# Value products of the first chunk ahead of the second gate pair in a decoder layer kernel: a change in the order of work

## Chip, cores and metric

One core of one Trainium2 chip runs the whole kernel. The metric is the time of one execution in microseconds, as the median of the runs; lower is better.

## What is computed

One decoder layer, in fp32, for a prompt of 256 tokens and eight sample sequences of one token each with 1024 cached tokens (8 pages of 128):

```
x = x + 0.5 * g1 * SwiGLU_1(mod1(rmsnorm(x)))
h = mod2(rmsnorm(x)); [qA|kA|vA|qB|kB|vB|gA|gB] = h @ w_in
  branch A: 8 heads x 64, blocks of 256, top-3 past blocks + own block
  branch B: 4 heads, q/k halves of 64, value 128, w = p0 - lam * p1, sub-RMSNorm
x = x + g2 * ((sig(gA) * yA + sig(gB) * yB) @ w_out)
x = x + 0.5 * g3 * SwiGLU_2(mod3(rmsnorm(x)))
```

In both branches the sample's token also attends to its own new key and value ("own products" below: q times own k). The model width is 1024, the feed-forward width 2816. The pages of keys and values are found through a table.

## The kernel before

Everything is held feature-major: 264 columns (256 prompt tokens and 8 sample tokens) by 1024 features in eight chunks of 128. A weight arrives in blocks of 1 MB in four buffers (`raw`). ScalarE rounds a half block to `whi` (the function `hi`), VectorE or GpSimd (POOL) computes the rest `wlo` (`lo`, L1055 on VectorE, L662 on POOL), and TensorE multiplies three times for each pair of 128x128 tiles: whi with hhi, whi with hlo, wlo with hhi (L1611 to L1613; in the later gates L1959 to L1961). A half block of 24 such products is one "half"; there are 20 halves from the keys and values to the first two gate blocks, numbered 0 to 19 (`kv_product(g)`, halves 16 to 19 are the gates' first two blocks, called W_GATE and W_GATE+1).

Every engine has its order of work written out by hand, and semaphores tie them together. The order around the change is this.

- **The loop over u = 0 to 16 on TensorE** computes half u, turns keys and values of earlier halves, and scores cached keys: `scores(0, u + 2)` for branch A and `scores(1, u)` for branch B, where one step is half a sequence (4 pages). Each needs its page block turned by VectorE in 32x32 tiles (`turn_keys`, L1266). At u = 12 it also multiplies the own products (tile `ev`, L1935) that VectorE made in `own_products` (L1294, L1299); the result goes into the sample's maxima.
- **VectorE beside it** turns the key blocks, and does the sample's softmax for two groups of four sequences, e = 0 and 1: `sample_logits` (block sums and distances), `sample_ranks` (the ranks of the blocks and the maximum, L1323 to L1348, after TensorE's `block_sums`, L1890), and, after ScalarE's exponentials (`sample_exp`, L868, L870) and TensorE's `exp_sums` (L1895), `sample_scale` (L1356 to L1363), which scales and turns the weights. TensorE turns them once more (`turn_probs`, L1904), and ScalarE copies them out (`turned_probs`) and into padded tiles (`pad_weights`, tile `wpad`, L952).
- **The loop over c = 0 to 7** has one chunk each: the cached values' products of one sequence (L1994; two half sequences of two branches, each 4 page products), the turn of the prompt's probabilities (L2022), the prompt's scores of the next chunk (L1910, L1911), halves of the later gates in chunks 1 to 6 (`gate_half`) and the prompt's output (L2044, L2045). VectorE has `prompt_logits` (L1376 to L1381) and `prompt_scale` (L1390 to L1401), ScalarE `prompt_exp` (L936, L938).
- **The page blocks** ("uses" 0 to 31, 16 of keys and then 16 of values, 1 MB for each branch and use) go through three buffers for each branch. SyncE (SP) loads branch A and the weights, POOL loads branch B (both L473). A load waits until the products of the use that had its buffer are done. The table `AHEAD` says behind which use SP asks for which weight block (L545).
- **POOL** also computes the rest of halves 5 to 19 in the same list as its loads.

Of the kernel before, what the change touches and what calls it, by code (L numbers as in the profile page):

```python
# [211 lines left out]
def build(nc, A, O):  # L212
    ctx = ExitStack()
    with ctx:
# [285 lines left out]
        def filler(k):  # L500

            return W_KV + k // 2, k % 2
# [7 lines left out]
        def turn_bank(c, h):  # L510
# [6 lines left out]
                 18: [W_GATE + 2, W_GATE + 3, W_GATE + 4], 19: [W_GATE + 5], 21: [W_GATE + 6], 23: [W_GATE + 7], 25: [W_BR]}  # L517
# [105 lines left out]
        def _(pool):  # L623
# [41 lines left out]
            for use in range(KVS + 2, 4 * TS):  # L665
                kv_load(pool, 1, use)
                if 6 <= use <= 11:
                    lo(*filler(use - 1))
                if 11 <= use < POOL_HALVES - 1:
                    lo(*filler(use))  # L670
                if use == POOL_HALVES - 2:
                    lo(*filler(use + 1))
                if use in K_ROWS:
                    i = K_ROWS[use]
                    pool.wait_ge(s_tok, 4 * (i + 1))
                    row_out("k", i // 2, i % 2, ktok, ktoks, s_krow)
                if use in V_ROWS:
                    i = V_ROWS[use]
                    pool.wait_ge(s_vtok, 4 * (i + 1))
                    row_out("v", i // 2, i % 2, vtok, vtoks, s_vrow)  # L680
# [15 lines left out]
        def _(a):  # L696
# [259 lines left out]
            for t in range(2):  # L956
                hi(W_GATE + 2, t)
# [3 lines left out]
            pad_weights(1)  # L961
            gate_pair(1)
            npp = 0
            sample_exp(1)
            for c in range(KC):
                gated = 1 <= c <= 6
                if c == 1:
                    turned_probs(1)
# [15 lines left out]
                if c + 1 < KC:  # L984
                    pad_weights(2 * c + 2)
                    pad_weights(2 * c + 3)
                    prompt_exp(c + 1)
                if gated:
                    gate_half(c + 1, 1)
# [55 lines left out]
        def _(v):  # L1045
# [432 lines left out]
            for c in range(KC):  # L1478
# [15 lines left out]
                if c == 0:  # L1494
                    sample_scale(1)
# [107 lines left out]
        def _(pe):  # L1603
# [309 lines left out]
            for u in range(2 * TS + 1):  # L1913
# [17 lines left out]
                if u == 12:  # L1931
# [31 lines left out]

            kv_product(17)
            kv_product(18)
            turn_probs(0)
# [13 lines left out]
            npp = 0  # L1980
            for c in range(KC):
# [5 lines left out]
                w0 = 24 - 8 * (c % 4)  # L1987
                for half in range(2):
                    pe.wait_ge(s_wpad, 2 * c + half + 1)
                    for ab in range(2):  # L1990
                        use = 16 + 2 * c + half
                        pe.wait_ge(kv_sem(ab, use), kv_landed(ab, use))
                        for q in range(4):
                            ins = mm(bank[32 * q:32 * q + 32, 4 + ab, :], wpad[half][:, q, ab, w0:w0 + 32], kv_slot(ab, use)[:, q, :],  # L1994
                                     start=(half == 0 and c % 4 == 0), stop=(half == 1 and q > 0 and c % 4 == 3))
                        ins.then_inc(s_pv, 1)
                    if half == 0 and c == 1:
                        turn_probs(1)
# [4 lines left out]
                    if half == 1 and c == 0:  # L2003
                        exp_sums(1)
# [7 lines left out]
                for h in range(2 if c < 4 else 1):  # L2012
# [4 lines left out]
                    if (c, h) == (0, 1):  # L2017
                        pe.wait_ge(s_sig, 2)
                    if (c, h) == (1, 1):
                        pe.wait_ge(s_pTs, 2)  # L2020
# [4 lines left out]
                if c + 1 < KC:  # L2025
                    pe.wait_ge(s_plog, 2 * c + 2)
                    if c == 0:
                        pe.wait_ge(s_sig, 1)
                    prompt_scores(c + 1)
# [16 lines left out]
                ins.then_inc(s_po, 1)  # L2046
                if c % 4 == 3:
# [86 lines left out]
```

## Time and profile before

| | |
|---|---|
| median of 3 runs | 769.61 us (768.85 to 771.45) |
| profiled execution: its time | 771.59 us |
| its span, first to last instruction | 769.9 us |
| mean granted TensorE clock | 0.984 |
| busy PE, DVE, ACT, POOL | 95%, 61%, 43%, 16% |
| read from HBM | 205.33 MB, 271 GB/s over the span |

The profile is of one execution. Busy shares are of its span, and positions in it are in microseconds from the span's start. A matmul's duration overlaps with its neighbours', so a group's cost is read from start to start. The stage that the change touches lies between about 360 and 450 us. A wait is shown behind an instruction in brackets: how long the engine was idle and who released it.

### The profile page before, as it was taken

The numbers are of one execution on the slowest core, as the hardware profiler recorded it, in microseconds if no ns is written. First come the engines' busy times: TensorE is split into PE (matmuls) and PEld (weight loads), VectorE is DVE, ScalarE is ACT, GpSimd is POOL, SyncE is SP. The second block draws the span as 40 slices with busy tenths as digits, with TensorE's granted clock in tenths as the row PEclk, the third lists the DMA queues.
The fourth block names the chain that finished last, engine by engine and source line by source line (L and its number), as shares of the span: only waits on it lengthen the run. The fifth ranks groups of instructions, "written<-read, shape, count | busy, mean of one in ns | idle before, by whom it ended". The sixth has DMA issues, their size and how long they took to land.

```text
span 769.9 us, 17290 instructions
## 1 busy us (share of the span) xinstructions
PE 734.7 (95%) x6732; PEld 654.3 (85%) x6732; DVE 467.9 (61%) x699; ACT 334.2 (43%) x568; POOL 123.7 (16%) x179
## 2 busy tenths in 40 slices
PE   5899999999999999998999699999989999999997
PEld 2398998999999799998886366669979999999997
DVE  2664445455354879978998255778676545545451
ACT  2453333344343643554255254475554434434431
POOL 0000000002000422787665223210000000000000
PEclk9999999999999999999899899999999999999999
DMA  9978989987986599999988998996517566555520
GB/s 353 375 245 271 323 288 317 331 263 293 393 273 203 234 391 381 375 389 390 368 315 280 404 401 300 356 346 224 165 55 218 165 184 193 168 172 183 185 91 29
DMA packets 116521, 209.57 MB, mean 272 GB/s; under 512 B 6714, under 2 KB 100186, under 8 KB 104162
## 3 DMA queue, kind: packets, MB, share of 16 engines
q1 hardware_dynamic: 106784, 159.47, 60.5%
q0 software_dynamic: 9440, 49.04, 16.4%
q8 instruction: 47, 0.77, 0.4%
q14 instruction: 24, 0.20, 0.1%
q10 hardware_dynamic: 226, 0.10, 0.0%
HBM read 205.33 MB, written 3.24 MB: 271 GB/s over the span
## 4 chain that ended last, share of the span: by engine, by line
PE 77%; DVE 11%; DMA 6%; issue 2%; ACT 2%; SPq 2%; ACTq 0%; DVEq 0%
PE bank L1611 21%; PE bank L1612 20%; PE bank L1613 20%; DMA early<-in_w_ada 3%; PE bank L1994 3%; PE bank L1860 2%; DMA kvA_lent<-in_cache_v_moba 2%; PE bank L1667 2%; PE bank L1959 1%; DMA kvA<-in_cache_k_moba 1%; PE bank L1960 1%; PE bank L1961 1%; DVE kvB L1266 1%; DVE wlo L1055 1%; SPq L473 1%
## 5 line engine op out<-in xcount | busy, mean ns | idle before, releaser
L1055 DVE TENSOR_TENSOR wlo<-raw,whi 128x1024 fp32r<-128x1024 f32 (+1 forms) x177 | 208.6, 1199 | 175.5 <-ACT whi L711 172.7
L1611 PE MATMUL bank<-hhi,whi 128*128 128x264 f32 x992 | 287.3, 290 | 3.6 <-DVE wlo L1055 2.0
L1612 PE MATMUL bank<-hlo,whi 128*128 128x264 f32 x992 | 282.6, 285 | 0.0
L1613 PE MATMUL bank<-hhi,wlo 128*128 128x264 f32 x992 | 282.0, 284 | 0.0
L711 ACT ACTIVATE whi<-raw 128x1024 fp32r<-128x1024 f32 (+1 forms) x192 | 194.5, 1034 | 105.8 <-PE bank L1613 70.4
L1611 PEld LDWEIGHTS bank<-hhi,whi 128*128 128x128 f32 x992 | 188.1, 190 | 15.9 <-issue 13.6
L1612 PEld LDWEIGHTS bank<-hlo,whi 128*128 128x128 f32 x992 | 188.3, 190 | 0.1
L1613 PEld LDWEIGHTS bank<-hhi,wlo 128*128 128x128 f32 x992 | 187.4, 189 | 0.0
L1611 PE MATMUL bank<-ahi,whi 128*128 128x264 f32 x416 | 119.8, 288 | 0.4 <-DVE alo L1569 0.4
L1613 PE MATMUL bank<-ahi,wlo 128*128 128x264 f32 x416 | 118.2, 284 | 0.0
L1612 PE MATMUL bank<-alo,whi 128*128 128x264 f32 x416 | 117.6, 283 | 0.0
L1611 PEld LDWEIGHTS bank<-ahi,whi 128*128 128x128 f32 x416 | 78.3, 188 | 0.8 <-DVE alo L1569 0.6
L1612 PEld LDWEIGHTS bank<-alo,whi 128*128 128x128 f32 x416 | 78.3, 188 | 0.2
L1613 PEld LDWEIGHTS bank<-ahi,wlo 128*128 128x128 f32 x416 | 78.3, 188 | 0.0
L745 ACT ACTIVATE sil<-bank 128x528 f32<-128x528 f32 x22 | 13.5, 612 | 74.5 <-PE bank L1613 74.5
L749 ACT ACTIVATE ahi<-act 128x528 f32 (+1 forms) x22 | 14.2, 646 | 53.8 <-DVE act L1141 53.8
L662 POOL TENSOR_TENSOR wlo<-raw,whi 128x1024 fp32r<-128x1024 f32 x15 | 35.8, 2388 | 1.9 <-ACT whi L711 1.3
L473 POOL DMA_DIRECT2D kvB<-in_cache_v_diff x44 | 23.3, 530 | 42.4 <-PE bank L1994 34.0
L1959 PE MATMUL bank<-hhi,whi 128*128 128x264 f32 x96 | 28.5, 297 | 0.0
L1145 DVE TENSOR_TENSOR alo<-act,ahi 128x528 f32 (+1 forms) x22 | 15.6, 709 | 19.3 <-ACT ahi L749 19.3
L1960 PE MATMUL bank<-hlo,whi 128*128 128x264 f32 x96 | 27.2, 284 | 0.0
L1961 PE MATMUL bank<-hhi,wlo 128*128 128x264 f32 x96 | 27.2, 283 | 0.0
(284 smaller groups left out, 825.6 us busy)
## 6 DMA issues: line engine op xcount, KB each, us to landing
raw<-in_ffn_w_gate SPq DMA_DIRECT2D x22, 1024.0 KB, 5.4
raw<-in_ffn_w_up SPq DMA_DIRECT2D x22, 1024.0 KB, 5.5
raw<-in_w_ada SPq DMA_DIRECT2D x20, 1024.0 KB, 7.0
raw<-in_w_in SPq DMA_DIRECT2D x20, 1024.0 KB, 10.6
raw<-in_ffn_w_down SPq DMA_DIRECT2D x16, 1024.0 KB, 5.1
kvA<-in_cache_v_moba SPq DMA_DIRECT2D x44, 256.0 KB, 6.3
kvB<-in_cache_v_diff POOLq DMA_DIRECT2D x44, 256.0 KB, 5.9
kvA<-in_cache_k_moba SPq DMA_DIRECT2D x36, 256.0 KB, 6.6
```

Of the source, the lines that this page charges most:

```text
L473: eng.dma_start(rows_, cache[bass.ds(page, 1)].rearrange("a (j t) d -> (a j) (t d)", t=4)).then_inc(kv_sem(ab, use), 16)
L662: nc.gpsimd.tensor_tensor(half_view(wlo[n % 2], key, t), half_view(raw[s], key, t), half_view(whi[n % 2], key, t).bitcast(F32), ALU.subtra ...
L711: nc.scalar.activation(half_view(whi[key[1] % 2], key, t), half_view(raw[s], key, t), ACT.Copy).then_inc(s_hi, 1)
L1055: dve.tensor_tensor(half_view(wlo[key[1] % 2], key, t), half_view(raw[s], key, t), half_view(whi[key[1] % 2], key, t).bitcast(F32), ALU.su ...
L1145: dve.tensor_tensor(alo[:, bass.ds(2 * i, 2), :], act[:, :, :], ahi[:, bass.ds(2 * i, 2), :].bitcast(F32), ALU.subtract).then_inc(s_alo, 1)
L1611: mm(out, wh, xh, start=start, stop=False)
L1612: mm(out, wh, xl, start=False, stop=False)
L1613: return mm(out, wl, xh, start=False, stop=stop)
L1959: mm(out, wh, hhi[:, k, :], start=(k == 0), stop=False)
L1960: mm(out, wh, hlo[:, k, :], start=False, stop=False)
L1961: ins = mm(out, wl, hhi[:, k, :], start=False, stop=(k == KC - 1))
L1994: ins = mm(bank[32 * q:32 * q + 32, 4 + ab, :], wpad[half][:, q, ab, w0:w0 + 32], kv_slot(ab, use)[:, q, :], start=(half == 0 and c % 4 == ...
```

## The change

It moves work in the lists of all engines; nothing is added or left out, but for one wait on POOL.

1. TensorE multiplies the own products at u = 13 instead of 12, behind half 13 and the turn of the values.
2. TensorE turns the first four sequences' weights right behind half 17, ahead of half 18, and does chunk 0's value products (a new function `values`) behind half 18, ahead of `block_sums(1)` and half 19.
3. In chunk 0 TensorE scores the prompt's second chunk between the two turns of the prompt's probabilities, and does `exp_sums(1)` last, behind the prompt's output.
4. The second four sequences' exponentials (ScalarE) stand behind the prompt's exponentials of chunk 1 instead of ahead of the loop; `sample_scale(1)` on VectorE stands in chunk 1 instead of 0; `turn_probs(1)` on TensorE in chunk 2 instead of 1, and ScalarE's copy too.
5. ScalarE rounds W_GATE+2 behind the padding of the weights instead of ahead of it.
6. POOL waits for the first scaled weights before it computes the rest of half 19.
7. Four blocks of gate and branch weights are asked for behind the page block that they stood ahead of.

```diff
-                 18: [W_GATE + 2, W_GATE + 3, W_GATE + 4], 19: [W_GATE + 5], 21: [W_GATE + 6], 23: [W_GATE + 7], 25: [W_BR]}
+                 18: [W_GATE + 2, W_GATE + 3, W_GATE + 4], 20: [W_GATE + 5], 22: [W_GATE + 6], 24: [W_GATE + 7], 26: [W_BR]}
...
                 if use == POOL_HALVES - 2:
+                    pool.wait_ge(s_pscaled, 1)
                     lo(*filler(use + 1))
...
             gate_pair(0)
-            for t in range(2):
-                hi(W_GATE + 2, t)
             turned_probs(0)
             a.wait_ge(s_wzero, 1)
             pad_weights(0)
             pad_weights(1)
+            for t in range(2):
+                hi(W_GATE + 2, t)
             gate_pair(1)
             npp = 0
-            sample_exp(1)
...
-                if c == 1:
+                if c == 2:
                     turned_probs(1)
...
                     prompt_exp(c + 1)
+                if c == 0:
+                    sample_exp(1)
...
-                if c == 0:
+                if c == 1:
                     sample_scale(1)
...
-                if u == 12:
+                if u == 13:
                     pe.wait_ge(s_ecur, 1)
...
+            def values(c, half):
+
+                w0 = 24 - 8 * (c % 4)
+                pe.wait_ge(s_wpad, 2 * c + half + 1)
+                for ab in range(2):
+                    use = 16 + 2 * c + half
+                    pe.wait_ge(kv_sem(ab, use), kv_landed(ab, use))
...
             kv_product(17)
+            turn_probs(0)
             kv_product(18)
-            turn_probs(0)
+            values(0, 0)
+            values(0, 1)
             block_sums(1)
             kv_product(19)
...
-                    if half == 0 and c == 1:
+                for half in range(2 if c else 0):
+                    values(c, half)
+                    if half == 0 and c == 2:
                         turn_probs(1)
...
-                    if half == 1 and c == 0:
-                        exp_sums(1)
...
                     if (c, h) == (0, 1):
+                        prompt_scores(1)
                         pe.wait_ge(s_sig, 2)
+                    if (c, h) == (1, 1):
+                        pe.wait_ge(s_pscaled, 2)
...
                 ins.then_inc(s_po, 1)
+                if c == 0:
+                    exp_sums(1)
```

The order of instructions shows it at three places. The first is TensorE behind half 18, before (L1904 is the turn of the weights, L1890 the block sums, the rows behind are half 19):

```order
L1613 MATMUL bank<-hhi,wlo_57 128x264
L1904 MATMUL bank<-prob_117,const 32x128 [waits probs_scaled]
L1904 MATMUL bank<-prob_117,const 32x128 x15
L1890 MATMUL bank<-sm,const 128x8 [waits block_parts]
L1611 MATMUL bank<-hhi,whi_55 128x264 [waits lo_ready,v_tokens_ready]
```

and now (L1974 are the value products, L1892 the block sums):

```order
L1615 MATMUL bank<-hhi,wlo_57 128x264
L1974 MATMUL bank<-kvA_97,wpad_142 32x512 [waits kv_landedA1,weights_padded]
L1974 MATMUL bank<-kvA_97,wpad_142 32x512 x3
L1974 MATMUL bank<-kvB_99,wpad_142 32x512 [waits kv_landedB1]
L1974 MATMUL bank<-kvB_99,wpad_142 32x512 x3
L1974 MATMUL bank<-kvA_lent,wpad_143 32x512 [waits kv_landedA2,weights_padded]
L1974 MATMUL bank<-kvA_lent,wpad_143 32x512 x3
L1974 MATMUL bank<-kvB_lent,wpad_143 32x512 [waits kv_landedB2]
L1974 MATMUL bank<-kvB_lent,wpad_143 32x512 x3
L1892 MATMUL bank<-sm,const 128x8 [waits block_parts]
L1613 MATMUL bank<-hhi,whi_55 128x264 [waits lo_ready,v_tokens_ready]
```

The turn is gone from here (it stands ahead of half 18), and eight rows of value products stand between half 18 and the block sums of the second four sequences.

The second is TensorE at the end of chunk 0, before (L1895 are the exponentials' sums, L2022 the turns of the prompt's probabilities, L1910 and L1911 the scores, L2044 and L2045 the output):

```order
L1994 MATMUL bank<-kvB_lent,wpad_143 32x512 x3
L1895 MATMUL bank<-sm,const 128x2 [waits probs_ready]
L2022 MATMUL bank<-const,plog_129 128x128 [waits prompt_probs]
L2022 MATMUL bank<-const,plog_129 128x128 x2
L2022 MATMUL bank<-const,plog_130 128x128 [waits gate_out,prompt_probs]
L2022 MATMUL bank<-const,plog_130 128x128 x2
L1910 MATMUL bank<-kT,qT 128x128 [waits gate_out,prompt_logits]
L1911 MATMUL bank<-kT,qT 128x256
L1910 MATMUL bank<-kT,qT 128x128
L1911 MATMUL bank<-kT,qT 128x256
L2044 MATMUL bank<-pts_131,vtok 64x256 [waits prompt_probs_ready]
L2045 MATMUL bank<-pts_131,vtok 64x128
```

and now (L1897 the sums, L2033 the turns, L1912 and L1913 the scores, L2053 and L2054 the output, L1974 chunk 1's values):

```order
L1912 MATMUL bank<-kT,qT 128x128
L1913 MATMUL bank<-kT,qT 128x256
L2033 MATMUL bank<-const,plog_130 128x128 [waits gate_out]
L2033 MATMUL bank<-const,plog_130 128x128 x2
L2053 MATMUL bank<-pts_131,vtok 64x256 [waits prompt_probs_ready]
L2054 MATMUL bank<-pts_131,vtok 64x128
L2053 MATMUL bank<-pts_132,vtok 64x256
L2054 MATMUL bank<-pts_132,vtok 64x128
L1897 MATMUL bank<-sm,const 128x2 [waits probs_ready]
L1974 MATMUL bank<-kvA_96,wpad_142 32x512 [waits kv_landedA0,weights_padded]
L1974 MATMUL bank<-kvA_96,wpad_142 32x512 x3
```

The sums, with their wait for the exponentials, have gone from the head of the chunk to its end, and chunk 1's values stand behind them.

The third is ScalarE in the same place, before (L868 and L870 are the second group's exponentials, L936 and L938 the prompt's):

```order
L925 ACTIVATE gT<-bank 128x528 [waits gemm_done]
L868 ACTIVATE prob_118,sm<-prob_118,mxt_123 128x256 [waits logits_ready]
L868 ACTIVATE prob_118,sm<-prob_118,mxt_123 128x256
L870 ACTIVATE ncur<-ncur 128x2
L983 ACTIVATE pts_131<-bank 128x384 [waits prompt_probs_turned]
L983 ACTIVATE pts_132<-bank 128x384 [waits prompt_probs_turned]
L952 ACTIVATE wpad_142<-probT_119 128x8x8 [waits v_used,probs_turned_ready]
L952 ACTIVATE wpad_143<-probT_119 128x8x8 [waits v_used,probs_turned_ready]
L936 ACTIVATE plog_129,stat<-plog_129,stat,qroot 128x128 [waits prompt_logits]
L938 ACTIVATE plog_129,stat<-plog_129,stat,qroot 128x256
L936 ACTIVATE plog_130,stat<-plog_130,stat,qroot 128x128 [waits prompt_logits]
L938 ACTIVATE plog_130,stat<-plog_130,stat,qroot 128x256
```

and now (L869 and L871, L937 and L939):

```order
L926 ACTIVATE gT<-bank 128x528 [waits gemm_done]
L983 ACTIVATE pts_131<-bank 128x384 [waits prompt_probs_turned]
L983 ACTIVATE pts_132<-bank 128x384 [waits prompt_probs_turned]
L953 ACTIVATE wpad_142<-probT_119 128x8x8 [waits v_used,probs_turned_ready]
L953 ACTIVATE wpad_143<-probT_119 128x8x8 [waits v_used,probs_turned_ready]
L937 ACTIVATE plog_129,stat<-plog_129,stat,qroot 128x128 [waits prompt_logits]
L939 ACTIVATE plog_129,stat<-plog_129,stat,qroot 128x256
L937 ACTIVATE plog_130,stat<-plog_130,stat,qroot 128x128 [waits prompt_logits]
L939 ACTIVATE plog_130,stat<-plog_130,stat,qroot 128x256
L869 ACTIVATE prob_118,sm<-prob_118,mxt_123 128x256 [waits logits_ready]
L869 ACTIVATE prob_118,sm<-prob_118,mxt_123 128x256
L871 ACTIVATE ncur<-ncur 128x2
```

The sample's exponentials have gone behind those of the prompt's second chunk.

## Rows read from the trace of the kernel before

**Rows 1.** The page's chain of work that ended last, shares of the span by engine

```profile
PE 77%; DVE 11%; DMA 6%; issue 2%; ACT 2%; SPq 2%; ACTq 0%; DVEq 0%
```

**Rows 2.** Windows: busy us (instructions) PE, PEld, DVE, ACT, POOL; PEclk, DMA share, GB/s

```profile
360.00:370.00 10.00, 6.32 (x57) 5.95 (x61) 9.96 (x12) 1.80 (x4) 7.24 (x10) 0.82 1.02 413
380.00:390.00 10.00, 9.94 (x129) 8.70 (x129) 9.65 (x16) 6.08 (x14) 9.86 (x13) 1.00 0.97 348
```

**Rows 3.** TensorE's timeline from 367 us: start, duration, instruction, [idle before, releaser]

```profile
367.32 1.86 PE L1935 MATMUL bank<-const,ev 128*128 128x1 f32 x8 [3.68 <-DVE ev L1299]
...
370.82 1.93 PE L1860 MATMUL bank<-kvB,qrow 128*32 128x128 f32 x32
372.68 0.59 PE L1611 MATMUL bank<-hhi,whi 128*128 128x264 f32 x1
```

**Rows 4.** VectorE's timeline from 365 us, same columns

```profile
365.00 1.38 DVE L1294 TENSOR_TENSOR stat<-qT,kT 128x32 f32<-128x32 f32 x2
...
381.04 2.67 DVE L1343 TENSOR_TENSOR mxt<-mxt,ncur 128x2 f32<-128x2 f32 x1
...
384.77 2.30 DVE L1266 STREAM_TRANSPOSE kvB<-kvB 128x2048 f32<-128x2048 f32 x1
```

**Rows 5.** POOL's timeline at 381 us, same columns

```profile
381.30 2.37 POOL L662 TENSOR_TENSOR wlo<-raw,whi 128x1024 fp32r<-128x1024 f32 x1
```

**Rows 6.** TensorE's timeline from 387 to 411 us

```profile
387.13 1.08 PE L1860 MATMUL bank<-kvB,qrow 128*32 128x128 f32 x32
...
398.06 1.08 PE L1904 MATMUL bank<-prob,const 128*32 128x128 f32 x32 [0.39 <-DVE prob L1360]
400.20 0.39 PE L1890 MATMUL bank<-sm,const 128*128 128x8 f32 x2 [1.05 <-DVE prob L1315]
...
405.06 1.06 PE L1994 MATMUL bank<-kvA,wpad 128*32 128x512 f32 x8
...
408.63 0.38 PE L1895 MATMUL bank<-sm,const 128*128 128x2 f32 x2
...
411.33 1.06 PE L1994 MATMUL bank<-kvA,wpad 128*32 128x512 f32 x8
```

**Rows 7.** VectorE's timeline from 401 to 415 us

```profile
401.38 0.16 DVE L1323 COPY sm<-bank 128x8 f32<-128x8 f32 x1
...
406.06 2.36 DVE L1055 TENSOR_TENSOR wlo<-raw,whi 128x1024 fp32r<-128x1024 f32 x2
...
411.69 0.73 DVE L1376 SCALAR_TENSOR_TENSOR plog<-const,qroot,bank 128x128 f32<-128x128 f32 x2
...
414.88 0.16 DVE L1381 SCALAR_TENSOR_TENSOR stat<-stat,qroot 128x2 f32<-128x2 f32 x1
```

**Rows 8.** ScalarE's timeline from 406 to 416 us

```profile
406.14 0.51 ACT L868 ACTIVATE prob<-prob,mxt 128x256 f32<-128x256 f32 x1 [0.36 <-DVE ncur L1348]
...
407.14 0.19 ACT L870 ACTIVATE ncur<-ncur 128x2 f32<-128x2 f32 x1
...
416.06 0.19 ACT L938 ACTIVATION_READ_ACCUMULATOR plog<-plog,stat,qroot 128x1 f32 x1
```

**Rows 9.** SyncE's timeline of transfer issues from 408 us

```profile
408.82 0.58 SPq L545 DMA_DIRECT2D raw<-in_w_in  x1
412.19 2.53 SPq L473 DMA_DIRECT2D kvA_lent<-in_cache_v_moba  x4
```

**Rows 10.** The chain of waits in order of time: start, duration, what

```profile
414.19 16.83 DMA kvA_lent<-in_cache_v_moba
431.15 3.64 PE bank L1994 x16
...
446.30 1.85 PE bank L1994 x16
```

**Rows 11.** Windows of one microsecond at two places, columns of rows 2

```profile
403.00:404.00 1.00, 1.00 (x7) 1.00 (x6) 0.93 (x3) 0.00 (x0) 0.00 (x0) 0.51 0.00 0
431.00:432.00 1.00, 0.85 (x5) 0.25 (x9) 0.00 (x0) 0.00 (x0) 0.00 (x0) 0.50 0.99 365
```

More of the change, by code:

```diff
@@ L1962, in gate_half @@
                 ins.then_inc(s_gemm, 1)
+            def values(c, half):
[4 more added lines that the diff above has]
+                    pe.wait_ge(kv_sem(ab, use), kv_landed(ab, use))
+                    for q in range(4):
+                        ins = mm(bank[32 * q:32 * q + 32, 4 + ab, :], wpad[half][:, q, ab, w0:w0 + 32], kv_slot(ab, use)[:, q, :],
+                                 start=(half == 0 and c % 4 == 0), stop=(half == 1 and q > 0 and c % 4 == 3))
+                    ins.then_inc(s_pv, 1)
             kv_product(17)
+            turn_probs(0)
             kv_product(18)
-            turn_probs(0)
+            values(0, 0)
+            values(0, 1)
             block_sums(1)
@@ L1980, in _ @@
             npp = 0
+            pe.wait_ge(s_plog, 2)
+            pe.wait_ge(s_sig, 1)
             for c in range(KC):
@@ L1986, in _ @@
                 gated = 1 <= c <= 6
[L1987 to L1996, printed above, removed]
-                    if half == 0 and c == 1:
+                for half in range(2 if c else 0):
+                    values(c, half)
+                    if half == 0 and c == 2:
                         turn_probs(1)
@@ L2017, in _ @@
                     if (c, h) == (0, 1):
+                        prompt_scores(1)
                         pe.wait_ge(s_sig, 2)
                     if (c, h) == (1, 1):
+                        pe.wait_ge(s_pscaled, 2)
+                    if (c, h) == (2, 1):
                         pe.wait_ge(s_pTs, 2)
@@ L2024, in _ @@
                     npp += 1
-                if c + 1 < KC:
+                if 1 <= c < KC - 1:
                     pe.wait_ge(s_plog, 2 * c + 2)
-                    if c == 0:
-                        pe.wait_ge(s_sig, 1)
                     prompt_scores(c + 1)
```

## Prediction

> **What bounds the kernel now.** I read the chain of waits of the page first: it follows TensorE for 77% of the span, VectorE for 11% and DMA for 6% [rows 1]. The change touches the mixing stage; the feed-forward stages before and after it are TensorE's own, and a microsecond won or lost in the stage should reach the end whole. So the question is what ends the waits in that stage.
>
> The windows come next [rows 2]: in the ten microseconds from 360 TensorE is busy 6.32 of 10 and VectorE 9.96; from 380 VectorE still has 9.65. In VectorE's timeline there is no idle entry at all from 352 to 408 us. TensorE's first wait, 3.68 us for the block-spread own products (tile ev), ends at 367.32 [rows 3]; what follows runs at the lower clock, thirty-two score products in 1.93 us, and the product at 372.68 still takes 0.59 us. But this wait is where TensorE catches up with VectorE, not what holds VectorE.
>
> VectorE's timeline says why [rows 4]: own products from 365.00, the last key block turned at 384.77, 2.30 us. In between a 128x2 maximum took 2.67 us at 381.04; a POOL subtraction of 128x1024 runs beside it from 381.30 for 2.37 us [rows 5], and the small operation ends when POOL's does. Six such operations stand between 365 and 397.
>
> From 387.13 TensorE is the slower one again [rows 6]: scores, three gate products, a wait of 0.39 us before the turn of the weights (398.06), one of 1.05 us before the block sums (400.20), then four value half-blocks from 405.06 to 408.63, and those of chunk 1 from 411.33.
>
> **Part 1: own products one step later, priced at nothing.** Eight small products move behind the next projection. TensorE no longer waits 3.68 us at 363.6, nor pays the low clock there. But the scores of the last key half wait for VectorE's turn that begins at 384.77 and ends at 387.07, and VectorE's list up to there is the same, with nothing in it that waited for TensorE. So I expect TensorE to reach those scores about 6 us early and to stand still until 387.1: the wait is moved, not removed. Its cover is that VectorE stays busy; bounds are a gain of 2.4 us (below, first rival) and a loss of 0.4 us, should POOL's earlier subtraction catch one more small operation.
>
> The moved wait costs something new. In the kernel before TensorE came to those scores at full clock (1.08 us [rows 6]). After six idle microseconds it will restart at half. The price comes from the other long wait of this trace: sixteen value products took 3.64 us behind it and 1.85 us elsewhere, and the half clock ended there, so 1.8 us. Bounds: 0, and 2.9 us, half of the 5.8 us from 367.32 to about 373.1. I take **+1.8 us**, since that wait was as long.
>
> **Part 2: turn and values ahead of the second gate pair's last half.** Before, 13.07 us pass from the scores (387.13) to the block sums (400.20). The waits of 0.39 and 1.05 go, since VectorE's scaled weights (398.0 before) now meet a TensorE that is 1.8 us later and still has a projection in between; the added wait on POOL keeps its last subtraction off that scaling, worth up to 2 us to VectorE, all of it hidden. Behind that wait in POOL's order stand the stores of value rows and the next page loads; those pages are read 20 us later, so nobody waits for them. Added ahead of the block sums are the values, 408.63 - 405.06 = 3.6 us. Block sums: 387.13 + 13.07 - 1.44 + 3.57 + 1.8 = **404.1**, 3.9 us later than before.
>
> **Part 3: the second four sequences' chain.** This is where it hurts. Behind the block sums VectorE has the ranks (401.38 to 406.06, 4.7 us), the low part of a gate weight (2.36 us) and now at once chunk 1's prompt logits (411.69 to 415.04, 3.35 us) [rows 7]. ScalarE then has the prompt's exponentials, ended 1.2 us later, and only behind them the sample's exponentials, 406.14 to 407.33, 1.2 us [rows 8]. The exponentials' sums on TensorE wait for that, and chunk 1's values stand behind them in TensorE's order. With 0.45 us for the block sums and 0.35 us for the sums: 0.45 + 4.7 + 2.36 + 3.35 + 1.2 + 1.2 + 0.35 = 13.6 us. So chunk 1's values start at 404.1 + 13.6 = **417.7**, against 411.33: 6.4 us later. TensorE has only some 6.5 us of work for these 13.6 (a projection, six turns, scores, prompt output), so it stands about 7 us and restarts at half clock once more, **+1.8 us** (bounds 0 and 2.9). ScalarE's two high parts of that weight also move, behind the padding; they are done before the ranks and cost nothing.
>
> **Part 4: pages earlier, weights later.** Before, SP issues a gate weight at 408.82 ahead of the value pages of 412.19 [rows 9], and TensorE stands 6.5 us until the last of those pages, 16.83 us on its way, is there at 431.02 (414.19 + 16.83); then come the 3.64 us at low clock [rows 10]. The granted clock was 0.51 at 403 to 404 and 0.50 at 431 to 432 [rows 11], the lower of the two levels (1.2 of 2.4 GHz); the first of these windows also shows the queues empty, 0 GB/s: no buffer was free. Now chunk 0's values free two pairs of buffers at about 402 and 404, and with no weight in front the page pair is issued at once: even with 16.8 us on its way it lands near 423. Both the 6.5 us and the 1.8 us of low clock go. The turn of the second probabilities (1.1 us) leaves chunk 1 and enters chunk 2: nothing. The later weights have at least a chunk until they are read: nothing.
>
> **Sum, at chunk 2's values.** Chunk 1 took 431.15 - 6.5 - 411.33 = 13.3 us. After: 417.7 + 13.3 - 1.1 + 1.8 = 431.7, against 431.15: +0.6. Behind it -1.8 (no low clock) and +1.1 (the turn): -0.1 us. **Five microseconds won at each end are spent in the middle: no change.** The profiled execution took 771.59 us (span 769.9), so 771.5 by its own clock; it stands 2.0 us above the median of the runs, 769.61, and I forecast for the median **769.5 us**.
>
> What this measurement can tell from no change is 0.3%, 2.3 us.
>
> **Rivals.**
> - *VectorE gets faster (0.31).* POOL's subtractions follow TensorE's scores through the buffers, so they come some 6 us earlier. Should one fall on the turn of the key block, which the subtractions do not lengthen (2.3 us with and without), instead of on the ranks, VectorE is 2.4 us earlier at 384.8, and everything behind with it: 769.5 - 2.4 = 767.1. For it: I place the subtraction for the eighteenth half at 381.5, one microsecond before the ranks would end unhindered. Against it: at 381.5 it hits. With full clock at the first restart as well, 765.3.
> - *The low clock lasts longer at both restarts (0.14).* If it ends as late as at 373.1 rather than as at 434.8, each restart costs 2.9 us instead of 1.8: 769.5 + 2.2 = 771.7, slower. It decides from where light products (scores, 32 columns) fill the first microseconds, as they do at the first restart; at the second, values of the kind that 3.64 us shows come first, which speaks against it there.
> - *The page wait moves one half on (0.10).* The next pages can only be asked for behind chunk 1's first values, 419.4 to 421.9. If the last of them is again 16.8 us on its way, it lands at 438.7; chunk 1 and the first half of chunk 2 need them at 431.7 + 1.8 + 1.1 + 3.0 = 437.6. A wait of 1.1 us and some low clock, 1.8 at most: 772.4, slower. It decides from 15.7 us on the way; against it, only some 5 MB will be asked for at that point at the 413 GB/s of [rows 2].
>
> **What would show it.** Right: TensorE idle about 6 us before the last key scores, which start within 0.5 us of 387; granted clock 0.5 behind it; block sums near 404; a wait of about 7 us before L1897 that ends on ScalarE's L871; no DMA wait at chunk 2's values, which start near 431.7. Wrong: key scores at 385 (VectorE faster, first rival), no wait at L1897 (my chain is too long), or a wait for kvA or kvB pages in chunk 2.

## The result, and the profile after

The changed kernel took 775.82 us (median of 7 runs, 772.82 to 777.81), the kernel before beside it 771.18 us (7 runs, 765.92 to 771.46). The ratio is 1.0068, with an interval of 1.0037 to 1.0098: slower by about 5 us, where no change was forecast (769.5 us, range 765.3 to 772.4). Timed once more later, it was 776.81 against 771.45 us (below), so the loss is the kernel's own.

The page's share line of the chain, of the changed kernel, answers to [rows 1]: DMA has gone from 6% to 3%, and TensorE from 77% to 82%.

```profile
PE 82%; DVE 11%; DMA 3%; ACT 2%; issue 2%; SPq 1%; ACTq 0%; DVEq 0%
```

TensorE's timeline of the changed kernel from 368 us (start, duration, instruction, [idle before, releaser]), beside [rows 3, 6]:

```profile
368.70 0.95 PE L1937 MATMUL bank<-const,ev 128*128 128x1 f32 x8
...
387.65 0.66 PE L1862 MATMUL bank<-kvB,qrow 128*32 128x128 f32 x8 [6.92 <-DVE kvB L1268]
...
401.50 1.07 PE L1974 MATMUL bank<-kvA,wpad 128*32 128x512 f32 x8
...
405.07 0.39 PE L1892 MATMUL bank<-sm,const 128*128 128x8 f32 x2
...
418.29 0.59 PE L1897 MATMUL bank<-sm,const 128*128 128x2 f32 x2 [6.70 <-ACT ncur L871]
418.81 1.93 PE L1974 MATMUL bank<-kvA,wpad 128*32 128x512 f32 x8
...
433.23 1.07 PE L1974 MATMUL bank<-kvA_lent,wpad 128*32 128x512 f32 x8
```

The picture is the one drawn in advance. The wait of 3.68 us before the own products (L1937, tile `ev`) is gone; one of 6.92 us stands before the last key scores. A wait of 6.70 us on ScalarE's L871 stands before the exponentials' sums. No wait for a page is left. Chunk 2's values start at 433.23, forecast 431.7. Behind the second wait eight value products take 1.93 us, against 1.07 us later on.

The windows of the changed kernel (columns of [rows 2]) show the granted clock in both waits, and again where the loop over the chunks ends:

```profile
386.00:387.00 1.00, 0.00 (x0) 0.00 (x0) 1.00 (x1) 1.00 (x6) 0.00 (x0) 0.50 1.03 387
414.00:415.00 1.00, 0.00 (x0) 0.00 (x0) 0.95 (x4) 0.64 (x3) 0.00 (x0) 0.50 1.09 442
505.00:512.00 7.00, 6.42 (x32) 3.68 (x22) 3.90 (x6) 3.75 (x6) 1.45 (x2) 0.74 0.94 332
512.00:519.00 7.00, 7.00 (x32) 6.82 (x33) 3.69 (x6) 4.79 (x7) 1.42 (x2) 0.52 0.93 339
```

and the last two windows in the kernel before, which [rows 11] did not hold:

```profile
505.00:512.00 7.00, 6.42 (x33) 4.72 (x32) 3.56 (x7) 4.13 (x9) 2.75 (x4) 0.84 0.94 305
512.00:519.00 7.00, 7.00 (x55) 7.00 (x55) 6.05 (x9) 4.43 (x7) 0.13 (x1) 0.91 1.00 364
```

The order of work there is the same in both kernels. Read in windows of one microsecond, the low clock lasts 10.2 us in the changed kernel (from 508 us) and 3.4 us in the kernel before (from 509 us). The forecast had not looked there.

To compare places I count from TensorE's branch B scores of half 11 (358.91 us before, 358.04 after), since executions enter the stage up to 4 us apart. The columns are microseconds from there; each comes from the starts in one profile. A chunk's column is the start of its value products, "page wait" the wait for a page in chunk 2, and "end" the end of the span.

| profile | last key scores | chunk 1 | chunk 2 | chunk 3 | end | page wait |
|---|---|---|---|---|---|---|
| before | 28.2 | 52.4 | 72.2 | 87.3 | 411.0 | 6.50 |
| before, 2nd | 28.3 | 52.5 | 69.7 | 84.5 | 409.7 | 3.89 |
| before, 3rd | 28.5 | 51.6 | 69.3 | 84.3 | 411.2 | 4.00 |
| change | 29.6 | 60.8 | 75.2 | 89.4 | 416.1 | none |
| change, 2nd | 29.6 | 60.8 | 75.2 | 89.5 | 416.1 | none |
| change, 3rd | 29.6 | 61.0 | 75.6 | 89.9 | 416.6 | none |

The kernel before differs from itself by 3 us at chunk 3, the changed one by 0.5 us. The profile that the forecast was worked out from is the kernel before with its longest page wait.

### The profile page after: what moved, and what is told of

It reads as the page before. It is cut to its first block, busy times and chain, and to the rows that moved or that the text cites. A ratio compares the mean times of both kernels' runs of the same rounds, so it can differ in the third digit from the quotient of the medians.

```text
span 774.1 us, 17290 instructions
## 1 busy us (share of the span) xinstructions
PE 736.2 (95%) x6732; PEld 655.5 (85%) x6732; DVE 468.6 (61%) x699; ACT 333.8 (43%) x568; POOL 123.4 (16%) x179
## 4 chain that ended last, share of the span: by engine, by line
PE 82%; DVE 11%; DMA 3%; ACT 2%; issue 2%; SPq 1%; ACTq 0%; DVEq 0%
PE bank L1613 22%; PE bank L1614 21%; PE bank L1615 21%; PE bank L1974 3%; PE bank L1862 3%; DMA early<-in_w_ada 3%; PE bank L1669 2%; PE bank L1961 1%; PE bank L1962 1%; PE bank L1963 1%; DVE wlo L1057 1%; DVE kvB L1268 1%; DVE prob L1342 1%; PE bank L2063 1%; DVE kvB_lent L1268 1%
## 5 line engine op out<-in xcount | busy, mean ns | idle before, releaser
L1613 PEld LDWEIGHTS bank<-hhi,whi 128*128 128x128 f32 x992 | 188.3, 190 | 16.5 <-issue 13.6
```

The costliest lines, as they stand in the source:

```text
L1613: mm(out, wh, xh, start=start, stop=False)
```

## The experiments

Two theories stood after the result, and the expectations call them A and B. **Theory A**: the loss lies in the stage, in TensorE's two new waits, in the chain on other engines that ends them, and in the restarts at low clock behind them. **Theory B**: the loss comes from the low clock at the end of the loop, whatever the stage does. The first four runs undo one part of the change each; the kernel before beside these four took 770.75 us (35 runs). "The change" is the first series, 775.82 us; it was not timed beside them, but the fourth run, as slow as the change, was.

### The sums later

`exp_sums(1)` leaves the end of chunk 0 and stands behind chunk 1's values.

```diff
+                if c == 1:
+                    exp_sums(1)
...
-                if c == 0:
-                    exp_sums(1)
```

> The changed kernel with the second group's exponential sums behind chunk 1's values instead of at the end of chunk 0. Theory A (the wait for them, 6.7 us, and the restart at half clock behind it are on the path): chunk 1's values start near 412 instead of 418.8, at full clock; 7 to 9 us faster than the changed kernel, less what the pages of use 20 and 21 then make TensorE wait; so 2 to 4 us faster than the kernel before. Theory B (the loss comes from the clock at the end of the loop, near 509 us, whatever the stage does): at most 2 us from the changed kernel, with a long low spell there again.

774.32 us (12 runs), ratio 1.0055 (1.0029 to 1.0082). Its timeline of TensorE:

```profile
426.41 0.88 PE L2035 MATMUL bank<-const,plog 128*128 128x128 f32 x3 [5.00 <-DVE prob L1362]
```

Chunk 1's values start 54.4 us after the reference score instead of 60.8, but chunk 2's at 73.8 instead of 75.2. The wait moved on to the next thing that needs VectorE's scaled weights, and kept 5.0 of its 6.7 us. The wait at the sums was the chain's, not the sums' own. Theory A's figure, 7 to 9 us faster, missed for that: 1.5 us came out, at chunk 3 too (88.0 instead of 89.4), and the low clock at the loop's end lasted 10.2 us again. By itself this run does not tell A from B.

### Block sums ahead of chunk 0's values

```diff
+            block_sums(1)
             values(0, 0)
             values(0, 1)
-            block_sums(1)
```

> The changed kernel with the second group's block sums ahead of chunk 0's values. Theory A: VectorE's ranks start 3.6 us earlier, the wait for the exponentials shrinks from 6.7 to about 3.1 us, and the restart may stay cold: 3 to 5 us faster than the changed kernel. Theory B: no change beyond 1 us in the stage's part, and the end of the loop decides.

772.65 us (12 runs), ratio 1.0026 (0.9999 to 1.0054): 3.2 us less than the change. The wait before the sums is 4.34 us instead of 6.70:

```profile
416.77 0.59 PE L1897 MATMUL bank<-sm,const 128*128 128x2 f32 x2 [4.34 <-ACT ncur L871]
```

The values had stood in the way of the chain that the next chunk waits for. Chunk 3's values start at 87.2 instead of 89.4, so 2.2 of the 3.2 us are seen in the stage, which theory B did not allow. By the medians this order is about two thirds of the loss; the interval, 0.9999 to 1.0054, is wide beside that.

### Own products back

```diff
-                if u == 13:
+                if u == 12:
```

> The changed kernel with the own products at step 12 as before. Theory A (VectorE sets when the last key scores start; the moved wait only costs a restart at half clock there): key scores still start near 387.5 but at full clock, so 1.5 to 2.5 us faster than the changed kernel. Rival (the move is a gain): 3 to 6 us slower.

772.6 us (12 runs), ratio 1.0027 (1.0 to 1.0053): 3.2 us less than the change too. Its last key scores come at 28.5 instead of 29.6 and at full clock (1.08 us), and chunk 3's values at 87.4 instead of 89.4. The two gains of 3.2 us together are more than the whole loss, so each is known only roughly.

### The old table of weights

The line of `AHEAD` as it was before.

> The changed kernel with the gate weights asked for as before. If the early values alone took the page wait away, no change (within 1 us) and no wait for kvA_lent at chunk 2. If the order of the queue did it, a wait of 3 to 7 us is back at chunk 2's values and the kernel is 3 to 8 us slower.

776.13 us (12 runs), ratio 1.0086 (1.0054 to 1.0119): as the change. Its profile, of the fastest of the twelve (771.59 us), has no page wait either, so the new table is not needed for that. Nor were the pages asked for earlier. SyncE's timeline here, beside 412.19 in the kernel before [rows 9]:

```profile
414.99 2.46 SPq L473 DMA_DIRECT2D kvA_lent<-in_cache_v_moba  x4
```

From the reference score that is 57.2 us, against 53.3 in the kernel before. But they landed 3.8 to 4.2 us after their issue, against 13.2 to 16.8 in the first profile of the kernel before, and TensorE came for them at 74.2, 2 us behind even the longest wait's end (72.2). With the early values the loads are spread otherwise; that this made them quick is likely and not shown by itself.

The next two do one part alone, from the kernel before (768.16 us beside them, 23 runs); both kernels were also profiled again there, unedited.

### The new table alone

> The kernel before with the new prefetch table alone. Page block 20 goes ahead of a weight of 1 MB. If the queue's order makes the page wait, it shrinks by 2 us or more, and the kernel is 1 to 5 us faster than before; if the wait comes from buffers that come free late, it stays, and the time is the same within 1 us.

769.31 us (12 runs), ratio 1.0008 (0.9983 to 1.0033): nothing. In its profile the page wait is 2.00 us and stands before another page, that of chunk 2's second half:

```profile
428.48 1.61 PE L1994 MATMUL bank<-kvA,wpad 128*32 128x512 f32 x8 [2.00 <-DMA kvA<-in_cache_v_moba]
```

The profile is of the fastest of the twelve (765.45 us): chunk 3's values start at 80.8 there, 3.5 us ahead of any profile of the kernel before. Its wait can't be laid against theirs as the table's doing. So neither expectation is met whole: the wait is another one, and the time is the same.

### Own products later, alone

> The kernel before with the own products one step later, alone. Theory A (VectorE sets when the last key scores start, so the wait only moves): a wait of about 6.9 us ahead of the last key scores in place of 3.7 us ahead of the own products, a restart at half clock behind it, and 1 to 3 us slower than before. Rival (a real gain): 3 us or more faster.

772.79 us (12 runs), ratio 1.0047 (1.0019 to 1.0075): 4.6 us above the kernel before beside it. The wait is the change's:

```profile
387.73 1.93 PE L1860 MATMUL bank<-kvB,qrow 128*32 128x128 f32 x32 [6.96 <-DVE kvB L1266]
```

Theory A had 1 to 3 us. The interval reaches from 1.5 to 5.8 us, and the profile shows less: chunk 3's values start at 85.3, within the 84.3 to 87.3 of the kernel before, and the span ends at 412.3. What is clear is that the last key scores come at 29.6 instead of 28.2 to 28.5, as in the change. The reason is on VectorE. The changed kernel there:

```profile
378.55 4.77 DVE L1342 TENSOR_TENSOR prob<-prob,sm 128x256 f32<-128x256 f32 x2
383.35 0.69 DVE L1344 TENSOR_REDUCE mxt<-prob 128x2 f32<-128x512 f32 x1
384.07 0.16 DVE L1345 TENSOR_TENSOR mxt<-mxt,ncur 128x2 f32<-128x2 f32 x1
...
385.29 2.31 DVE L1268 STREAM_TRANSPOSE kvB<-kvB 128x2048 f32<-128x2048 f32 x1
```

with POOL beside it:

```profile
378.52 2.13 POOL L473 DMA_DIRECT2D kvB_lent<-in_cache_v_diff  x4
380.67 2.35 POOL L662 TENSOR_TENSOR wlo<-raw,whi 128x1024 fp32r<-128x1024 f32 x1
```

and the same two products in the kernel before, with POOL's load beside them and the subtraction that follows the one of 381.30 [rows 5]:

```profile
379.40 0.89 DVE L1340 TENSOR_TENSOR prob<-prob,sm 128x256 f32<-128x256 f32 x2
...
379.02 2.26 POOL L473 DMA_DIRECT2D kvB<-in_cache_v_diff  x4 [0.86 <-PE bank L1860]
...
387.06 2.40 POOL L662 TENSOR_TENSOR wlo<-raw,whi 128x1024 fp32r<-128x1024 f32 x1
```

The two subtractions near 381 us are not of the same half. POOL makes fifteen, for halves 5 to 19. In the kernel before, 381.30 is the twelfth, of half 16, and 387.06 that of half 17; in the changed kernel 380.67 is the thirteenth, of half 17. So the subtraction of half 17 came 5.5 us earlier, counted from the reference score (28.15 to 22.63), and took the place in time that half 16's had held (22.39). VectorE's two products of L1342 now end with it: 4.77 us instead of 0.89. The maximum behind them falls from 2.67 us [rows 4] to 0.16, so the net is 1.4 us on the turn of the key block. All three profiles of the change show 4.77 or 4.78 us, and this one 4.50; with the own products back it is 0.89. The subtraction by itself, 2.35 us, costs no more than in the kernel before; what is new is that VectorE is held from about 379.0, 1.7 us before it begins. POOL was issuing a page load then, but the kernel before had such a load beside the same products (379.02 to 381.28) and they were not held. What held them in the change stays open.

### The kernel before, again

> The kernel before, once more under the profiler. If the wait of 6.5 us for value pages at chunk 2 belongs to the kernel, it is here again, 5 us or more. If it was a matter of that one execution, it is under 3 us here, and the change then has little to give back at that place, which would explain most of the 5 us that it costs.

770.38 us. Neither expectation came: the page wait is between the two, and the low clock behind it lasts 3.4 us, where the first profile has 6.8:

```profile
428.71 1.93 PE L1994 MATMUL bank<-kvA_lent,wpad 128*32 128x512 f32 x8 [3.89 <-DMA kvA_lent<-in_cache_v_moba]
```

### The change, again

> The changed kernel once more under the profiler. The waits ahead of the last key scores (6.9 us) and ahead of the exponentials' sums (6.7 us) come from the order of the work and stand here within 0.3 us. The low clock behind chunk 7 (508 to 518 us) is expected to differ in length if it depends on where in the execution it falls, and to be 10 us again if it belongs to the order.

780.05 us. It entered the stage 4.1 us later than the first profile and then kept its pace to 0.1 us (table above), with waits of 6.96 and 6.71 us. Between these two profiles the stage is not where the changed kernel varies. The low clock at the loop's end lasts 10.2 us again.

### All that helped, together

From the change: own products at u = 12, block sums ahead of chunk 0's values, the exponentials' sums behind chunk 1's first values and gate half, and, not tried alone, VectorE's `sample_scale(1)` in chunk 0 ahead of its next low part.

```diff
-                if c == 1:
-                    sample_scale(1)
...
+                if c == 0:
+                    sample_scale(1)
...
-                if u == 13:
+                if u == 12:
...
+            block_sums(1)
             values(0, 0)
             values(0, 1)
-            block_sums(1)
...
+                    if half == 0 and c == 1:
+                        exp_sums(1)
...
-                if c == 0:
-                    exp_sums(1)
```

> The changed kernel with four of its steps put otherwise: own products at step 12 again, the second block sums ahead of chunk 0's values, the exponentials' sums inside chunk 1 (behind the first gate half), the second scaling on VectorE ahead of the next weight's low part. By theory A (chain behind the block sums, and the restarts) nothing waits 6.7 us any more: counted from the score product of half 11, chunk 3's values start at 79 to 81 us (84.5 and 87.3 in the kernel before, 89.4 in the changed one), and the kernel is 3 to 6 us faster than before. By the rival (the early values themselves cost the time) it is no faster than before.

764.18 us (6 runs, 762.27 to 765.65) against 770.87 us, ratio 0.991 (0.9887 to 0.9934): **faster than both kernels**, 11.6 us below the change. TensorE's timeline has one long wait left in the stage, the old one for `ev`, and 1.56 us before the turn of the weights:

```profile
366.29 1.83 PE L1937 MATMUL bank<-const,ev 128*128 128x1 f32 x8 [3.68 <-DVE ev L1301]
...
395.61 1.08 PE L1906 MATMUL bank<-prob,const 128*32 128x128 f32 x32 [1.56 <-DVE prob L1362]
```

Chunk 2's values start 64.9 us after the reference score, 4.4 to 7.3 us ahead of the kernel before. Chunk 3's are at 79.1, inside theory A's 79 to 81; the rival, that the early values themselves cost the time, falls. So a kernel with the early values can be faster than the kernel before, once the work around them stands otherwise. How much of the 6.7 us is theirs, and how much is that of VectorE's earlier scaling, no run separates.

### POOL's wait left out

```diff
-                    pool.wait_ge(s_pscaled, 1)
```

> The changed kernel without POOL's added wait. Both theories: VectorE's scaling may be held 2 us by POOL's last subtraction, but TensorE comes to the turn of the weights later than that, so no change within 1 us, and the same waits of 6.9 and 6.7 us.

776.69 us (12 runs, one of which took 1440.17 us for a cause not known and is left out of the ratio), ratio 1.0072 (1.0049 to 1.0095): as the change. POOL's last subtraction starts only when ScalarE has rounded:

```profile
396.84 2.39 POOL L662 TENSOR_TENSOR wlo<-raw,whi 128x1024 fp32r<-128x1024 f32 x1 [1.33 <-ACT whi L711]
```

and VectorE's scaling was done by 393.1, so here the wait would have had nothing to hold.

### Work in the waits, too much of it

To price the restarts, TensorE gets products of constants into a bank that is overwritten afterwards, ahead of the last key scores and of the exponentials' sums, 14 in each. They are added work and part of no result.

```diff
+                if u == 15:
+                    pe.wait_ge(s_vtok, 10)
+                    for _ in range(14):
+                        mm(bank[:, 0, :], C("ones"), const[:, 0:512], start=True, stop=True)
...
                 if c == 0:
+                    for _ in range(14):
+                        mm(bank[:, 3, :], C("ones"), const[:, 0:512], start=True, stop=True)
                     exp_sums(1)
```

> The changed kernel with 14 products of constants in each of the two long waits of TensorE (ahead of the last key scores, and ahead of the exponentials' sums), written to a bank that nobody reads; they add work that the kernel does not need. The waits themselves stay, now filled. If restarting at half clock costs what the first profile shows, scores and values behind them run at full clock (1.08 us and 1.06 us instead of 1.94 and 1.93), and the kernel is 3 to 5 us faster than the changed one, that is about as fast as before. If the clock behind the waits costs nothing, no change within 1 us, or 1 us slower.

781.06 us (5 runs), ratio 1.013 (1.0104 to 1.0155). The 14 products took 12.2 us, not the 7 us of the wait:

```profile
380.77 12.18 PE L1944 MATMUL bank<-const 128*128 128x512 f32 x28
392.88 1.08 PE L1862 MATMUL bank<-kvB,qrow 128*32 128x128 f32 x32
```

The key scores started 5 us late for that, so this run says nothing of the price: mine was the mistake, an fp32 product of 512 columns is two records of 0.44 us each, start to start.

### The kernel before, a third time

> The kernel before a third time under the profiler. The page wait at chunk 2's values was 6.5 and 3.9 us in the two profiles so far. If it varies with the execution, a third value, between 0 and 7 us; the other waits (3.7, 0.4 and 1.05 us) stand within 0.1 us.

771.63 us, page wait 4.00 us. The other waits are 3.68, 0.53 and 1.05 us, so all but the second stand within 0.1 us. Of the three profiles only the first has more than 4 us at the page.

### Work in the waits, of the right size

The same with `range(7)` in both places, so 6.1 us of work in waits of 6.9 and 6.7; the change beside it, unedited, and the kernel before at 771.45 us (23 runs).

> The change with 7 instead of 14 products of constants in each of TensorE's two long waits, so 6.1 us of work (in the run with 14 they took 12.2 us) in waits of 6.9 and 6.7 us. If the two restarts at half clock cost about 2.5 us each, the last key scores start near 387.7 as in the change, both low stretches behind the waits are gone, and the time is some 4 to 6 us below the change beside it. If the low clock costs nothing and only the waits count, the two low stretches go and the time stays within 1 us of the change beside it.

771.43 us (12 runs), ratio 1.0007 (0.9981 to 1.0033). TensorE's timeline:

```profile
382.83 6.17 PE L1944 MATMUL bank<-const 128*128 128x512 f32 x14
389.93 1.08 PE L1862 MATMUL bank<-kvB,qrow 128*32 128x128 f32 x32 [0.93 <-DVE kvB L1268]
...
411.66 6.28 PE L2062 MATMUL bank<-const 128*128 128x512 f32 x14
418.45 0.38 PE L1897 MATMUL bank<-sm,const 128*128 128x2 f32 x2 [0.51 <-ACT ncur L871]
418.76 1.07 PE L1978 MATMUL bank<-kvA,wpad 128*32 128x512 f32 x8
```

and its windows in the waits and behind the loop:

```profile
388.00:389.00 1.00, 1.00 (x3) 0.17 (x1) 1.00 (x1) 1.00 (x6) 0.00 (x0) 1.00 0.97 377
416.00:417.00 1.00, 1.00 (x4) 0.46 (x3) 0.74 (x4) 0.85 (x3) 0.00 (x0) 1.00 0.95 390
505.00:512.00 7.00, 6.42 (x28) 5.37 (x26) 2.31 (x6) 2.45 (x7) 1.18 (x2) 0.65 0.89 297
512.00:519.00 7.00, 7.00 (x52) 6.91 (x52) 6.04 (x8) 4.48 (x7) 0.97 (x2) 0.86 0.98 378
```

The key scores stand at 29.6 from the reference score, as in the change: what they wait for comes no earlier. But the clock is 1.00 now in and behind both waits, chunk 3's values start at 85.1 instead of 89.9 beside it, and seven products of no use in each wait make the kernel 5.4 us faster than the change beside it (0.9981 to 1.0033 against 1.0036 to 1.0079).

### The change, a third time

> The change again, unedited, timed beside the run with products of constants in its waits. If the loss of 5 us is the kernel's own, it is 0.4 to 0.9% slower than the kernel before here too. If it was the chance of one chip or hour, it falls within 0.3%. In its profile the low clock near 508 us lasts 7 to 10 us if that belongs to the change, 3 us as in the profile of before if it is a matter of the execution.

776.81 us (12 runs), ratio 1.0058 (1.0036 to 1.0079). The stage repeats (table above), and so does the low clock at the loop's end, 10.2 us long.

## Why the prediction was wrong

Point by point, with the places counted from the reference score, so that the forecast's 387.1, 404.1, 417.7 and 431.7 are 28.2, 45.2, 58.8 and 72.8.

- **Part 1, the moved wait**: right in kind and size (6.92 us, about 6 forecast). **Failed: "priced at nothing".** The key scores come at 29.6, 1.4 us late, since the products of L1342 now end with POOL's subtraction. The bound that I gave for this, a loss of 0.4 us, was too small by a factor of three. It allowed for one more small operation held while a subtraction runs; it did not allow for a hold that begins 1.7 us before the subtraction, and that is the part which costs. The Trainium skill (GPSIMD Engine Reference, Key points) says that GpSimd and VectorE contend where VectorE's instruction has two SBUF inputs or runs in a mode that uses two ports. The rows agree in kind: L1342 in the change and the maximum in [rows 4], which have two inputs, were held, and a turn of a key block (2.26 us at 368.57, beside a subtraction from 368.72 to 371.11) was not.
- **The first restart**, 1.8 us: from the key scores to the turn of the weights the change takes 9.73 us, with the clock kept 7.58 us, so 2.15 us. Block sums at 47.0 instead of 45.2: 1.4 us from the late key scores and 0.35 from the restart.
- **Part 3, the chain**: right; 13.74 us from the block sums to chunk 1's values, 13.6 forecast. So were its order and its last link, ScalarE's L871. Chunk 1 at 60.8.
- **The second restart**, 1.8 us: chunk 1 takes 14.42 us, with the clock kept 12.39 us, so 2.0 us. Chunk 2 at 75.2 instead of 72.8; one chunk on, 89.4 against a forecast of 87.2. Both restarts together were sized 3.6 us and measured 4.2: too small by 0.6.
- **Part 4, the page wait: failed in the size of what was removed.** It did go, but the 6.5 us and the full 1.8 of low clock were those of one execution. The other two profiles waited 3.89 and 4.00 us and stood 2.8 and 3.0 us earlier at chunk 3. Averaged over the three, the kernel before is there at 85.4 and not at 87.3. I had seen that the profiled execution stood 2.0 us above the median, and shifted the forecast with it as a whole. The page wait alone doesn't make that difference: the third profile waited 4.00 us and took 771.63 us, as long as the first. It lost behind chunk 3 what it had won before it (next point). The pages' way was sized right for the kernel before and not for the change: 4.7 to 7.1 us there, where I had allowed the 16.8 of the row; nothing hung on it.
- **"A microsecond won or lost in the stage should reach the end whole": failed by a little.** From chunk 3 to the end the changed kernel took 326.7, 326.6 and 326.8 us, the kernel before 323.7, 325.2 and 326.9: 1.4 us more on average. This follows the low clock in that stretch before the span's last microseconds, read in windows of one microsecond: 10.2 us in all three profiles of the change; 3.4 and 6.8 in the first two of the kernel before, and 6.8 and another 3.4 near 460 us in the third. Each 3.4 us went with 1.5 to 1.7 us. The run with the old table has the changed kernel's stage, yet 3.4 us of low clock and 323.7 us, so a length of 10.2 is not fixed by the stage's order.

Sum, on the averages of three profiles each: at chunk 3 the change is 2.4 us later than forecast (89.6 instead of 87.2) and the kernel before 1.9 us earlier than I had it (85.4 instead of 87.3); less the 0.1 that was forecast and with 1.4 behind it, that makes 5.6, the difference of the ends (416.3 and 410.6). The medians differ by 4.6 to 5.4. All three profiles of the kernel before are of executions of 770.4 to 771.6 us, while its runs go from 764 to 775; no shorter one was profiled. Why the low clock behind the loop is as long as it is stays open. With the clock kept in both waits it lasted 6.8 us, as in two profiles of the kernel before: one profile doesn't settle it.

**The rivals.** The first (VectorE faster) had its premise right: the subtractions came some 6 us earlier, and that of the eighteenth half (number 17) stood where I had placed it, 22.63 us from the reference score, that is 381.5 on the clock of the profile before. What I held against it came true: it hit the ranks. But it hit more than a small operation, and VectorE was 1.4 us later, not 2.4 earlier. The second (each restart 2.9 us, 771.7) named the right side; measured were 2.15 and 2.0. The run that keeps the clock shows how much hangs on the restarts: without them the change stands where the kernel before does. But 3.6 of these 4.2 us were in the forecast, so they are not what it missed. The third (page wait one half on) did not happen in the change; the new table alone has a wait of 2.00 us at that place. That is nearer the former, but no weight stood ahead of them, so it does not test the rule. The wait on POOL and the later weights cost nothing, as said; ScalarE's later rounding was not tried by itself.

What the text had right besides is its complaint in Part 3, that the chain is where it hurts. It stopped at that price and didn't ask whether the values needed to stand ahead of the block sums: that order costs 2.2 us in the stage and 3.2 us by the medians, most of the 3.6 us that the values take.

## What to carry to other kernels

A wait that one execution shows has a size for that execution: before a sum takes all of it away, look at a second profile, above all where the wait is for a DMA; the profile's distance from the median does not tell which term is long. When work is pulled forward on the engine that everyone waits for, put it behind the instruction that starts a chain on other engines, not ahead of it. And a wait of 7 us on TensorE costs the wait and about 2 us behind it; where such a wait can't be removed, products of no use inside it bought those back here, as long as they fit into it: twice as many made the kernel slower.

## What the runs showed of the hardware

- Two restarts at the lower of TensorE's clock levels (granted 0.50, that is 1.2 of 2.4 GHz) behind idle stretches of 6.9 and 6.7 us cost 4.2 us in the stage, read against the same stretches with seven constant products in each wait (granted 1.00).
- Two VectorE products of 128x256, 0.89 us together, took 4.77 us and ended 0.3 us behind POOL's 128x1024 subtraction of 2.35 us. The hold began before the subtraction is shown to begin (379.0 against 380.67 us). POOL was issuing a page load then, and its spans in a profile are rough; the same products beside such a load in the kernel before took their 0.89 us.
- From one execution to another the stretch behind chunk 3 took 323.7 to 326.9 us, by the length of its low clock: 3.4 to 10.2 us.
- Three executions of one kernel waited 6.50, 3.89 and 4.00 us for the same page, while the two waits between engines in the changed kernel repeated within 0.05 us over three.
